# A linear-attention mixer's weighted sums, with fp32 products written as three fp32r products

## The reference

```python
q_dec = qc * exp(b);  k_inv = kc * exp(-b);  k_end = kc * exp(b_last - b)   # b: running sum of log decays
scores = einsum('bhncd,bhnsd->bhncs', q_dec, k_inv)
o_intra = einsum('bhncs,bhnse->bhnce', where(mask, scores, 0.0), vc)
o_t = q_t S_{t-1};  S = S * diag(dl) + k_t^T v_t                            # between the chunks
o = rmsnorm(o_forward + o_backward, o_norm)
return (o * silu(g_out)) @ w_out
```

## Time and profile before

| | us |
|---|---|
| median of 3 runs | 2176.5 (2176.48 to 2177.87) |
| span of the profiled execution | 2174.5 |
| PE busy | 2146.3 (99%) |
| VectorE busy | 1515.7 (70%) |
| ScalarE busy | 1192.1 (55%) |
| GpSimd busy | 220.4 (10%) |

### The profile page before, as it was taken

How to read it: one execution, slowest core, us unless ns; L and a number is a source line. 1 busy time by engine, 2 the same in 40 slices (tenths; PEclk the granted TensorE clock), 3 DMA queues, 4 the chain that set the end, 5 groups by cost and what they waited for, 6 DMA issues and landing times.

```text
span 2174.5 us, 38978 instructions
## 1 busy us (share of the span) xinstructions
PE 2146.3 (99%) x14559; PEld 1988.1 (91%) x14559; DVE 1515.7 (70%) x2075; ACT 1192.1 (55%) x1788; POOL 220.4 (10%) x146
## 2 busy tenths in 40 slices
PE   9999999999999999999999999999999999999998
PEld 8888899999889999999988889999889999999987
DVE  6676765668578888888855556999666565567755
ACT  5455654545455545555544446555666565676553
POOL 0000000000003223232300000221000000012110
PEclk9999999999999999999999999999999999999999
DMA  8655566657656576666666665665345647555454
GB/s 292 198 156 162 160 202 209 198 171 238 213 157 205 182 220 187 210 198 188 217 200 204 203 202 171 195 191 189 118 118 179 183 142 235 171 160 146 136 203 156
DMA packets 259011, 405.59 MB, mean 187 GB/s; under 512 B 16671, under 2 KB 115868, under 8 KB 257852
## 3 DMA queue, kind: packets, MB, share of 16 engines
q1 hardware_dynamic: 257204, 396.87, 58.8%
q10 hardware_dynamic: 1688, 7.07, 0.9%
HBM read 396.32 MB, written 4.22 MB: 184 GB/s over the span
## 4 chain that ended last, share of the span: by engine, by line
PE 90%; DVE 5%; ACT 3%; issue 1%; DMA 0%; DVEq 0%; ACTq 0%; SPq 0%
PE bank L2304 29%; PE bank L2300 23%; PE bank L2413 14%; PE bank L2297 12%; PE bank L2896 3%; PE bank L2319 2%; DVE wboth L1388 1%; ACT wboth L706 1%; PE bank L2643 1%; PE bank L2865 1%; PE bank L2821 1%; PE bank L2615 1%; DVE xtok L1542 0%; PE bank L2681 0%; PE bank L2348 0%
## 5 line engine op out<-in xcount | busy, mean ns | idle before, releaser
L1388 DVE TENSOR_TENSOR wboth<-raw,wboth 128x1024 fp32r<-128x1024 f32 (+1 forms) x748 | 909.2, 1228 | 516.5 <-ACT wboth L706 513.5
L706 ACT ACTIVATE wboth<-raw 128x1024 fp32r<-128x1024 f32 (+1 forms) x748 | 770.8, 1039 | 609.9 <-PE bank L2300 263.5
L2300 PE MATMUL bank<-aboth,wboth 128*128 128x512 f32 x2496 | 812.8, 382 | 2.3 <-DVE aboth L1607 1.1
L2297 PE MATMUL bank<-aboth,wboth 128*128 128x256 f32 x2496 | 659.2, 274 | 1.0 <-DVE wboth L1388 1.0
L2304 PE MATMUL bank<-aboth,wboth 128*128 128x272 f32 (+1 forms) x5184 | 624.0, 280 | 4.6 <-DVE aboth L1607 3.1
L2304 PEld LDWEIGHTS bank<-aboth,wboth 128*128 128x128 f32 x5184 | 606.1, 190 | 8.4 <-issue 3.9
L2300 PEld LDWEIGHTS bank<-aboth,wboth 128*128 128x128 f32 x2496 | 462.4, 190 | 59.9 <-issue 1.6
L2297 PEld LDWEIGHTS bank<-aboth,wboth 128*128 128x128 f32 x2496 | 478.4, 192 | 12.6 <-issue 2.7
L2413 PE MATMUL bank<-wboth,ghi 128*128 128x512 f32 x704 | 210.0, 380 | 0.9 <-DVE wboth L1388 0.9
L2924 POOL CAST ghi<-pr 128x256 f32 x44 | 84.3, 1917 | 691.2 <-DVE pr L1876 691.2
L2413 PEld LDWEIGHTS bank<-wboth,ghi 128*128 128x128 f32 x704 | 133.3, 189 | 19.9 <-DVE wboth L1388 1.3
(11 more groups left out here) (373 smaller groups left out, 1874.3 us busy)
## 6 DMA issues: line engine op xcount, KB each, us to landing
raw<-in_w_up SPq DMA_DIRECT2D x176, 512.0 KB, 4.6
raw<-in_w_in SPq DMA_DIRECT2D x156, 512.0 KB, 4.5
raw<-in_attn_w_in SPq DMA_DIRECT2D x96, 512.0 KB, 4.1
raw<-in_gla_w_in SPq DMA_DIRECT2D x96, 512.0 KB, 3.9
raw<-in_w_down SPq DMA_DIRECT2D x80, 512.0 KB, 4.6
raw<-in_w_out SPq DMA_DIRECT2D x32, 512.0 KB, 4.3
raw<-in_attn_w_out SPq DMA_DIRECT2D x32, 512.0 KB, 3.9
raw<-in_gla_w_out SPq DMA_DIRECT2D x32, 512.0 KB, 4.1
```

The source lines that it names most:

```text
L706: act.activation(whi[:, u % RING, 0:c], raw[:, u % RAW, 0:c], ACT.Copy).then_inc(whi_ready, 1)
L1388: dve.tensor_tensor(wlo[:, u % RING, 0:c], raw[:, u % RAW, 0:c], whi[:, u % RING, 0:c].bitcast(F32), ALU.subtract).then_inc(wlo_ready, 1)
L2297: mm = pe.matmul(bank[:, base + t, 0:T], w[1][:, k, col:col + P], in_turns(rhs(0, k0 + k)), start=False, stop=False)
L2300: mm = pe.matmul(bank[:, base + t, 0:2 * T], w[0][:, k, col:col + P], parts_in_turns(both(k0 + k)), start=first, stop=last)
```

## The change

The four heads' fp32 products of values and scores become three fp32r products each, read in turns; the small product with `scm` is read in turns too.

- The values are split: ScalarE copies a head's `v3` (128 x 2 x 512) to `v3_high` four steps before the head, VectorE subtracts into `v3_rest` three steps before. `v3_rest` stands in the place of `v3`, `v3_high` in that of the head's part of `cum`.
- The scores are split at lag 2: ScalarE copies `sc` (128 x 512) to `sc_high`, VectorE subtracts into `sc_rest`, in the place of `sc`. TensorE's sums at lag 3 wait for it (`low_made`).
- The results in PSUM are now interleaved, so the product with the gate reads `osq3` untwined.
- The input's load from DRAM waits for the fourth head's sums, as `cum` is in use until then.

```diff
+        sc_high = sb("sc_high", [P, 2, TB], F32R, at_=tmp_at + 2 * T2 * 4 + 64)
+        v3_high = sb("v3_high", [P, 2, 8 * T2], F32R, at_=cum_at)
+        sc_rest = sb("sc_rest", [P, 2, TB], F32R, at_=sc_at)
+        v3_rest = sb("v3_rest", [P, 2, D], F32R, at_=R2 + 4 * 16 * T2)
...
+        def head_values(t, h):
+            return t[:, :, 2 * h * T2:2 * h * T2 + GL_V] if t is v3_high else t[:, :, h * GL_V:(h + 1) * GL_V]
...
+            sp.wait_ge(o3_ready, GL_HEADS)
...
+                if lag == -4:
+                    act.wait_ge(v3_taken, 3 * h + 3)
+                    act.wait_ge(e_q, 2 * h + 2)
+                    act.wait_ge(e_k, 2 * h + 2)
+                    act.wait_ge(e_dec, 2 * h + 2)
+                    act.activation(head_values(v3_high, h), head_values(v3, h), ACT.Copy).then_inc(high_made, 1)
+                if lag == 2:
+                    act.wait_ge(sc_ready, 3 * h + 3)
+                    if h:
+                        act.wait_ge(o3_ready, h)
+                    act.activation(sc_high[:, :, :], sc[:, :, :], ACT.Copy).then_inc(high_made, 1)
...
+                if lag == -3:
+                    dve.wait_ge(high_made, 3 * h + 1)
+                    dve.tensor_tensor(head_values(v3_rest, h), head_values(v3, h), head_values(v3_high, h).bitcast(F32), ALU.subtract)\
+                       .then_inc(low_made, 1)
+                if lag == 2:
+                    dve.wait_ge(high_made, 3 * h + 3)
+                    dve.tensor_tensor(sc_rest[:, :, :], sc[:, :, :], sc_high[:, :, :].bitcast(F32), ALU.subtract).then_inc(low_made, 1)
...
-                        z = gg[:, 4 * h:4 * h + 4, :]
-                        dve.tensor_tensor(z, osq3[:, :, :], z, ALU.mult).then_inc(z3_ready, 1)
+                        z = halves_of(gg[:, 4 * h:4 * h + 4, :])
+                        dve.tensor_tensor(z, untwined_of(osq3[:, :, :]), z, ALU.mult).then_inc(z3_ready, 1)
...
-                    pe.wait_ge(sc_ready, 3 * h + 3)
-                    pe.wait_ge(scm_low, h + 1)
+                    pe.wait_ge(low_made, 3 * h + 3)
...
                         for k in range(2):
-                            pe.matmul(o, v3[:, k, col:col + P], sc[:, k, :], start=k == 0, stop=False)
-                        mm = pe.matmul(o, v3m[0:64 + TM, col:col + P], scm[0:64 + TM, :], start=False, stop=True)
+                            values_of = [head_values(t, h)[:, k, v * P:(v + 1) * P] for t in (v3_high, v3_rest)]
+                            for vp, sp_ in PASSES:
+                                pe.matmul(o, values_of[vp], in_turns((sc_high, sc_rest)[sp_][:, k, :]), start=(k, vp, sp_) == (0, 0, 0),
+                                          stop=False)
+                        mm = pe.matmul(o, v3m[0:64 + TM, col:col + P], in_turns(scm[0:64 + TM, :]), start=False, stop=True)
```

More of the change, by code:

```diff
@@ L285, in two_blocks_kernel @@
         dec = sb("dec", [P, 2, 2, 4], F32, at_=tmp_at + 2 * T2 * 4)
+        sc_high = sb("sc_high", [P, 2, TB], F32R, at_=tmp_at + 2 * T2 * 4 + 64)
+        v3_high = sb("v3_high", [P, 2, 8 * T2], F32R, at_=cum_at)
+        sc_at = R2 + 4 * (16 * T2 + 3 * D + KD * TB + 2 * P + T2 + 8 * T2 + 8 * TB + 2 * T2 + 2 * TB + 2 * 240 + 2 * 192)
+        sc_rest = sb("sc_rest", [P, 2, TB], F32R, at_=sc_at)
+        v3_rest = sb("v3_rest", [P, 2, D], F32R, at_=R2 + 4 * 16 * T2)
         gate_at = R2 + 4 * (16 * T2 + 3 * D + KD * TB + 2 * P + T2 + 2 * 4 * T2)
@@ L415, in two_blocks_kernel @@
             sem, "m_root m_mean m_rstd m_scaled m_made m_hi m_ready".split())
-        v_low, pT_low, scm_low, up_hi, up_lo = map(sem, "v_low pT_low scm_low up_hi up_lo".split())
+        v_low, pT_low, low_made, up_hi, up_lo = map(sem, "v_low pT_low low_made up_hi up_lo".split())
         s_ready, s_biased, max_ready, max_sink, p_ready, sink_ready, sum_sink, inv_sum, p_second, p_scaled, \
@@ L439, in two_blocks_kernel @@
             sem, "x_parked x_back up_clear z_sum z_abs z_min z_exp z_ln z_sub cum_ready v3_turned v3_taken".split())
-        e_q, e_k, e_d, e_dec, d_sub, q_dec, k_inv, k_end, k_far, sc_sum, x_sum, xm_sum, sc_part, sc_own, sc_ready, scm_ready, \
+        e_q, e_k, e_d, e_dec, d_sub, q_dec, k_inv, k_end, k_far, sc_sum, x_sum, xm_sum, sc_part, sc_own, sc_ready, high_made, \
             o3_ready, o3_sq, o3_sum, o3_root, o3_rstd, o3_scaled, z3_ready, z3hi = map(
-                sem, "e_q e_k e_d e_dec d_sub q_dec k_inv k_end k_far sc_sum x_sum xm_sum sc_part sc_own sc_ready scm_ready "
+                sem, "e_q e_k e_d e_dec d_sub q_dec k_inv k_end k_far sc_sum x_sum xm_sum sc_part sc_own sc_ready high_made "
                      "o3_ready o3_sq o3_sum o3_root o3_rstd o3_scaled z3_ready z3hi".split())
@@ L1311, in head_step @@
                     act.activation(scm[0:TM, :], bank[0:TM, 6, 0:TB], ACT.Copy)
-                    act.activation(scm[32:32 + TM, :], bank[0:TM, 6, 0:TB], ACT.Copy).then_inc(scm_ready, 1)
+                    act.activation(scm[32:32 + TM, :], bank[0:TM, 6, 0:TB], ACT.Copy).then_inc(high_made, 1)
                 if lag == 3:
@@ L2176, in head_step @@
                                     bank[64:P, 5, TB:TB + P].rearrange("p (t c) -> p t c", t=2)).then_inc(sc_ready, 1)
-                    dve.wait_ge(scm_ready, h + 1)
+                    dve.wait_ge(high_made, 3 * h + 2)
                     dve.tensor_tensor(scm[64:64 + TM, :], bank[0:TM, 6, 0:TB], scm[0:TM, :].bitcast(F32), ALU.subtract)\
-                       .then_inc(scm_low, 1)
+                       .then_inc(low_made, 1)
                 if lag == 4:
```

## The result

| | us |
|---|---|
| median before, measured beside it | 2176.5 (2176.45 to 2177.87) |
| median after | 2185.67 (2184.22 to 2185.89) |
| ratio after to before | 1.0039, 95% interval 1.0028 to 1.0049 |
| predicted | 2179.3, range 2175.5 to 2182.9 |

A forecast was written before the change was run, and what follows sets the result against it. The prediction took TensorE, busy 99% of the span, as the bound. Three stalls of 2.02 less four gains of 0.81 gave +2.8 us, from a median of 2176.5 to 2179.3, range 2175.5 to 2182.9.

The forecast's parts named there:

- PE's gain: Last mixer's weighted sums: 3.13 us instead of 3.94 a head, so 0.81 saved, 3.24 for four.
- The wait for sc_rest: Before the sums of heads 0, 1 and 2, PE stalls 2.02 us each; no stall before head 3.
- Its chain: Ahead of the sums: exponentials, then sc_high to 1974.94, sc_rest to 1976.01 beside GpSimd, PE starting at 1976.06.
- the other end: At sc_rest: rival without exclusion between VectorE and GpSimd, stall 1.68 us a head, +1.8 in all; chance 0.12.
- The lock didn't go to GpSimd twice: Rival at sc_rest: GpSimd's first kinv product goes before it, PE waits 1.2 us longer in three heads, +6.4; chance 0.12.
- The margin of 0.2 us in head 1: Ahead of head 1's score copies: the values' split fits into VectorE's wait for PE with 0.2 us left.
- TensorE falls to the lower of its two clock levels after a stall: Rival behind the new stalls: a unit at 1.2 GHz takes 2.7 us more after each, +10.8 in all; chance 0.03.
- between 1945 and 1960 PE was idle for 1.46 of 15 us, and the granted clock is 1.00: Row of an existing stretch, cited in the clock rival: clock at the 2.4 GHz level, 2.0 us idle not far from that.
- The values' split ... these cost only if VectorE then reaches the score copies late: Copy and subtraction four and three steps before the head: hidden by VectorE's waits for PE, costed at nothing.
- The gated product, "I take nothing ... the other heads have room": VectorE's strided read of osq3: costed at nothing; twice as long would make only head 1 late, by some 1.0 us.
- no stall: Rival at the sums: PE doesn't wait for the scores' split and its gain remains, 2173.3 us, -0.15%; chance 0.07.
- a stall of 1.0 instead of 2.0 a head: Before the sums: the shorter stall given as reason for the range's lower end, 2175.5 us.

The follow-up runs named there:

- e4: Kernel after the change, but GpSimd's products by the keys for the next head wait until sc_rest is made; 2183.55 us.
- e6: As e2, with GpSimd's two kinv products of a head held until VectorE has added the squares of the head before; 2174.69 us.
- e12: The kernel of e6 run once more, unchanged, in more rounds; 2174.68 us.
- e8: Kernel after the change, splits kept, but PE's sums read tiles that lie ready and don't wait for sc_rest; 2177.31 us.
- e1: Kernel after the change, with the scores' split put ahead of the reversed loop, so ahead of the next head's exponentials and to_ends; 2177.9 us.
- e2: As e1, with head 0's v3_rest on VectorE also moved from lag -3 to lag 1; 2177.11 us.
- e7: Kernel before, with only the sums changed to products read in turns from tiles that lie ready, nothing split; 2174.84 us.
- e11: Kernel after the change run once more, unchanged, on the chip of the runs beside it; 2184.13 us.
- e9: Kernel after the change, with 4 products of constants on PE ahead of head 0's far scores, so later waits move; 2187.67 us.
- e10: Kernel after the change, with 8 products of constants on PE ahead of head 0's far scores, so later waits move; 2186.25 us.
- e5: Kernel after the change, with the sums in their old fp32 form, reading the tiles of the two rests; 2186.58 us.

## Why the prediction was wrong

Right, with their sizes:
- PE's gain: 0.80 us a head, predicted 0.81. The sums took 3.14 and 3.13 where the clock stayed.
- The wait for sc_rest before heads 0, 1 and 2 and none before head 3: 2.07, predicted 2.02. Its chain was right in each link: sc_high behind the four exponentials, sc_rest 1.04 by exclusion (1.68 without it was the other end; e4, where GpSimd is silent, gave 1.72), kinv lengthened behind it. The lock didn't go to GpSimd twice.
- The margin of 0.2 us in head 1: VectorE still waits 0.15 us for PE ahead of head 1's score copies, where it waited 1.57.

Wrong (of the 6.4 us that the forecast lacks, the first three make up 5.07, 0.89 and 0.33):
- **"TensorE falls to the lower of its two clock levels after a stall", given 0.03.** This rival was the case, and the largest term missing: 1.69 us in each of three heads, 5.07 in all, where the rival itself said 2.7 a head. The step that failed is the inference "between 1945 and 1960 PE was idle for 1.46 of 15 us, and the granted clock is 1.00": that row speaks for a wait of 1.46 and says nothing for 1.90. Of the wait at 1952 it is still true in every profile taken here. But one execution's row doesn't show what the next will do, as e6 and e12 show after waits of 1.10, and length is no safe guide: a wait of 1.83 at 102.58 left the clock at 1.00 in the trace of before and in all others. For the waits of 2.0 that the prediction itself made it had no row of the clock behind them, and should have carried both ends of that, as it did for the other costs.
- **"The values' split ... these cost only if VectorE then reaches the score copies late", costed at nothing.** The cover was looked up for one reader. v3_rest of head 0 also stands ahead of values_low of v3m on VectorE (1965.46), for which PE's far scores wait: 0.89 us. The rule that the prediction followed for ScalarE, to list all that is queued behind the new instruction, wasn't followed here.
- **The gated product, "I take nothing ... the other heads have room".** Head 3 has no room: its gated product takes 1.57 us instead of 1.22, and the last projection comes 0.33 later. The stride alone isn't the reason: in heads 0 to 2 of e8 the strided product takes 1.22, as before. What lengthens it (1.31 in after's heads 0 to 2, too) stays open.
- One more term would have come in had the big wait not hidden it: the squares against kinv cost 0.8 to 1.0 us a head in e1, e2 and e8, where the sums don't wait for sc_rest behind the exponentials and kinv stands where it was (0.36 in e7, which has no split). So the change's full gain of 3.2 us was not to be had by taking away the wait for sc_rest alone, which the rival "no stall" assumed; e1 and e2 show it.
- A slip without effect: "a stall of 1.0 instead of 2.0 a head" gives 3 x 1.0 - 3.24 = -0.2, so 2176.3, not 2175.5 as the lower end of the range.

Open: what decides whether the clock falls after a wait (below), and a part of the 0.8 us between the stage of e6 and e12 (-2.76) and their medians (-2.0 and -1.9): 0.33 of it is the later end named above, and falls of the clock elsewhere move single runs by about 1 us.

## What to carry to other kernels

A new wait on an engine that was never idle can have two prices: its own length, and what the engine does at a lower clock behind it. One profile doesn't settle the second, since the same kernel paid it in one execution and not in another; carry both, and see whether the waiter can be fed before it is freed. Before calling an instruction hidden, list everything queued behind it on its engine with each one's reader, in the very unit where it stands, and for two-input work on VectorE also what GpSimd will be doing by then. In a loop that takes heads in reverse, a step added at the end of a head stands behind the next head's whole preparation: put it ahead of the loop, as e6 does.

## What the runs showed of the hardware

- A PE wait of 1.9 us was followed by a granted clock of 0.50 in 11 of 15 cases: 3 of 3 in after, 2 of 3 in e11 (the same program), 3 of 3 in e9, 2 of 3 in e10, 1 of 3 in e5. After e4's waits of 1.6 it stayed at 1.00, 3 of 3, and so it did in all 14 profiles after the waits of 1.5 at 1952, of 1.6 at 1601 and of 1.83 at 102.6 (times of before). Yet waits of 1.10, each about 1 us after one of 0.7, were followed by 0.50 in 2 of 14 profiles at 621 and in 2 of 14 at 1765. No threshold of length follows from this. In after the granted clock falls 0.8 to 0.9 us behind the end of the wait; in e10's head 1 it falls 0.15 us behind. The clock is back before the 28 products are done in each of after's heads, with PE busy all the time.
- The Trainium skill (TensorE: Matmul & The Clock Gate, "What's actually happening") says that the gate follows how busy the array was of late and isn't aligned with the start of the kernel. That one program keeps its clock in one execution and loses it in another, as after and e11 do in head 0 (4.83 and 3.21 us), agrees with that; no run here was made to show the alignment itself.
- VectorE and GpSimd exclude each other instruction by instruction, whichever is there first: sc_rest 1.04 instead of 0.69, the squares 1.67 (e2) and 1.46 (e8) instead of 0.69 (e6), and kinv 3.57 to 3.97 instead of 2.53 (e6) for two.
